# Turning the queries and keys of two attentions through device memory instead of on TensorE

## The chip, the cores and the metric

One NeuronCore of a Trainium2 chip runs the whole program. The metric is device time in microseconds (us) of one execution. The kernel before takes 820.13 us (median of 3 runs, 819.89 to 820.23).

The engines named below are TensorE (PE in the profile; PEld is its weight load), VectorE (DVE), ScalarE (ACT), GpSimd (POOL) and SyncE (SP), which here only starts transfers. Each works through its own list of instructions in order and waits on semaphores.

## The reference, cut to what matters

Two layers of a decoder trunk over 256 tokens of width 2048. Each normalises its input, multiplies it by one wide matrix, feeds the slices of the product to four mixers and multiplies their gated outputs by `w_out`:

```python
for l in range(DEPTH):                       # DEPTH = 2
    u = _rmsnorm(x, ln_g[l]) @ w_in[l]       # 2048 x 6232
    y_a = _gla(...) * silu(g_a)
    y_b = _ssd_mixer(...)
    y_c = _mla(...) * silu(g_c)              # 4 heads, queries and keys of 128 + 64 (the 64 with rope)
    y_d = _dilated_attention(...) * silu(g_d)  # 4 heads of 128, queries and keys with rope
    x = x + concat[y_a, y_b, y_c, y_d] @ w_out[l]
```

Both attentions normalise queries and keys per head, then compute `softmax(mask(q @ k.T * scale)) @ v`, causally, over 256 keys. All data is float32. The queries and keys are made with tokens on the 128 partitions, while the score matmul contracts over the 128 columns of a head, so it needs them turned: columns on partitions, tokens along the free axis.

## The kernel before

**Units.** Both big products run in float32 accuracy from float32r pieces: a weight block is split into `w_hi` (rounded) and `w_lo` (the rest), the activations likewise, and three of the four products are summed in PSUM (`gemm`). The weights come in 144 units per layer, numbered n = 0 to 143 (8 units make one block of 512 or 278 output columns), with 4 more units for the attention's own projections. For each unit four things happen: SP starts a load of 512 KB into one of 4 buffers `raw` (L527); ScalarE copies it to `w_hi` (L1025; "hi n" below); VectorE subtracts for `w_lo` (L1386; "lo n"); TensorE does 8 matmuls with `w_hi` (L702, L703) and 4 with `w_lo` (L711). The load of unit n is started when lo n-4 is done, and hi n waits until TensorE has used unit n-4.

**Everything else is threaded between units.** All other work is written between two units of each engine at a fixed n: `PE_AT` gives n for TensorE's jobs (after unit n), and code of the form `if n == 88:` for the others. The tables `ORDER` name the steps of each engine in order, so that a step can wait for "step X of engine Y". Two pairs of PSUM banks (`pairs`) are used in turn by TensorE's jobs (`bank`), and `LAST_READER` says whose reading frees a pair.

**The attentions.** For the first attention ("mla"), VectorE scales the heads (`mla n`, L1628) and does the rope on the 64-wide part (`mla rope`); then TensorE turns four query heads ("mla qT", after unit 85), four key heads ("mla kT", 86) and the rope parts ("mla rT", 87), each as 8 transposes of 128x128 into PSUM (L874), which ScalarE copies to SBUF (L1213). After unit 89 come the scores of two heads ("mla S 0", L885 and, for the rope part, L891). VectorE takes mask and maximum ("mla max 0", L1659; "mla nmax 0", L1663), ScalarE the exponential ("mla P 0", L1221), TensorE turns the probabilities after unit 92 ("mla PT 0", L900), and TensorE multiplies by the values; so on for the other two heads and for the second attention ("dil"), whose queries and keys are turned after units 95 and 97 and whose first scores come after unit 99. "gated" and "evac 10" belong to the gate of another mixer that passes through at the same place: evac 10 is ScalarE's gate activation with two table loads, directly ahead of ScalarE's copy for "mla rT".

**Turning through memory.** Another way to turn exists already, for the mixers' outputs (`y_squares`) and the state-space output (`ssd_y_squares`): VectorE transposes each 32x32 square in place of its block (`turn_squares`, two instructions for 128x1024, L1355), SP writes the 512 KB to device memory (`squares_out`, L509, at unit at+5) and reads it back in 4 pieces of 128 KB (`squares_back`, L516, at unit at+7), which puts the squares where a full transpose would have them. `SQUARES` names each such tensor with the buffers and its unit "at".

Of the kernel before, what the change touches and what calls it, by code (L numbers as in the profile page):

```python
# [186 lines left out]
for _n in range(8):  # L187
# [3 lines left out]
          "mla kv 1": KV_AT, "ssd Y": 76, "mla qT": 85, "mla kT": 86, "mla rT": 87, "mla S 0": 89, "mla PT 0": 92,  # L191
          "mla S 1": 93, "mla O 0": 94, "dil qT": 95, "mla PT 1": 96, "dil kT": 97, "mla O 1": 98, "dil S 0": 99,
# [7 lines left out]
               "mla cT": ("dve", "mla cT"), "mla qT": ("act", "mla qT"), "mla kT": ("act", "mla kT"), "mla rT": ("act", "mla rT"),  # L200
               "dil qT": ("act", "dil qT"), "dil kT": ("act", "dil kT")}
LAST_READER |= {f"gla level {n}": ("dve", f"gla merge {n}") for n in range(1, 8)}
LAST_READER |= {f"mla {w} {t}": ("act", f"mla {w} {t}") for w in ("q", "kv") for t in range(2)}
for _m in ("mla", "dil"):
    for _i in range(2):
# [25 lines left out]
        "mla cT, ssd Y, mla qT, mla kT, mla rT, "  # L231
        "mla S 0, mla PT 0, mla S 1, mla O 0, dil qT, mla PT 1, dil kT, mla O 1, dil S 0, dil PT 0, dil S 1, dil O 0, "
# [6 lines left out]
        "evac 8, mla kv 0, mla kv 1, mla rs 1 sum, dil rs 0 sum, evac 9, dil rs 1 sum, mla qT, mla kT, evac 10, "  # L239
        "mla rT, mla P 0, ssd rs sum, mla PT 0, mla P 1, evac 11, dil qT, mla PT 1, dil kT, dil P 0, dil PT 0, "  # L240
# [7 lines left out]
        "mla n 0 0, mla n 0 1, ssd yT, mla n 1 0, ssd y squares, mla n 1 1, mla rope products, mla rope, dil n 0 0, dil n 0 1, "  # L248
        "dil n 1 0, dil n 1 1, dil rope 0 products, dil rope 0, dil rope 1 products, dil rope 1, gated 1, mla max 0, "
# [10 lines left out]
def build(nc, xT_d, x_d, pos_d, cols_d, w_d, params_d, gla_w2, gla_b,  # L260
          consts_d, masks_d, out_d):
    ctx = ExitStack()
    with ctx:
# [142 lines left out]
        mqT, mkT = two(A(0, 1024), 4), two(A(1024, 1024), 4)  # L406
# [9 lines left out]
        dqT, dkT = two(A(5632, 1024), 4), two(A(6656, 1024), 4)  # L416
# [87 lines left out]
        def _(sp):  # L504
# [15 lines left out]
            for l in range(DEPTH):  # L520
                for g, n in enumerate(STREAM):
# [109 lines left out]
        def _(pe):  # L631
# [15 lines left out]
            for l in range(DEPTH):  # L647
# [268 lines left out]
                def mla_qT():  # L916
                    pe.wait_ge(*dve("mla rope"))
                    heads_T("mla qT", lambda t, h: mqk[:, t, h, 0:P])

                def mla_kT():  # L920
                    heads_T("mla kT", lambda t, h: mqk[:, t, 4 + h, 0:P])

                def mla_rT():
                    rr = mrr.rearrange("p t (a b) d -> p t a (b d)", b=2)
                    heads_T("mla rT", lambda t, h: rr[:, t, h])
# [3 lines left out]
                       "mla qT": mla_qT, "mla kT": mla_kT, "mla rT": mla_rT}  # L929

                def stages(n):
                    for name in PE_AT:
# [9 lines left out]
                        elif name == "dil qT":  # L942
                            pe.wait_ge(*dve("dil rope 1"))
                            heads_T(name, lambda t, h: dqk[:, t, h])
                        elif name == "dil kT":
                            heads_T(name, lambda t, h: dqk[:, t, 4 + h])
# [38 lines left out]
        def _(act_):  # L985
# [23 lines left out]
            for l in range(DEPTH):  # L1009
# [38 lines left out]
                def evac(b):  # L1048
# [180 lines left out]
                for place, n in enumerate(STREAM):  # L1229
# [72 lines left out]
                    if n == slot("mla qT"):  # L1302
                        heads_T("mla qT", mqT)
                    if n == slot("mla kT"):
                        heads_T("mla kT", mkT)
                    if n == slot("mla rT"):
                        heads_T("mla rT", mrT.rearrange("p a b s -> p (a b) s"))
                    if n == slot("dil qT"):
                        heads_T("dil qT", dqT)
                    if n == slot("dil kT"):  # L1310
                        heads_T("dil kT", dkT)
# [14 lines left out]
        def _(v):  # L1326
# [37 lines left out]
            for l in range(DEPTH):  # L1364
# [329 lines left out]
                for place, n in enumerate(STREAM):  # L1694
# [87 lines left out]
                    for i in range(2):  # L1782
# [72 lines left out]
```

## Time and profile before

| | us |
|---|---|
| median of 3 runs | 820.13 |
| profiled execution | 820.42 |
| its span, first to last instruction | 818.6 |
| TensorE busy in it | 812.2 (99%) |
| VectorE busy | 606.6 (74%) |
| ScalarE busy | 477.2 (58%) |

The granted TensorE clock is at full speed throughout. The span is the time from the first instruction to the last one of the profiled execution; 1.8 us of its device time lie around it. Busy times of TensorE's matmuls overlap, since they are pipelined: how long a job holds the engine is read from the starts of what stands before and behind it. In a row of the timeline the first number is the start, the second the duration of the row (several instructions in a row are merged), and a bracket at its end says how long the engine was idle before it and what ended the wait.

### The profile page before, as it was taken

Reading aid. Unit: us, or ns where it says so; the run is one execution under the profiler, and the core shown is the slowest. Engines: PE = TensorE matmul, PEld = TensorE weight load, DVE = VectorE, ACT = ScalarE, POOL = GpSimd, SP = SyncE. Lnnn points to the kernel's source line nnn. Section 1 sums busy time; section 2 is a strip of 40 time slices with the busy share of each in tenths; the row PEclk is TensorE's granted clock in tenths of the full one; section 3 lists DMA queues with packets and bytes.
Section 4 is the critical chain, followed back from the end, with each engine's and each line's share of the span. In section 5 each row is a group of like instructions: output and inputs, shape, how many; then the busy total and the mean of one; then the engine's idle time right before and its main releaser. Section 6 shows DMA issues by size and latency. Waiting matters only on the chain.

```text
span 818.6 us, 11315 instructions
## 1 busy us (share of the span) xinstructions
PE 812.2 (99%) x4212; PEld 689.6 (84%) x4212; DVE 606.6 (74%) x1074; ACT 477.2 (58%) x786; POOL 52.8 (6%) x64
## 2 busy tenths in 40 slices
PE   8999999999999999999999999999999999999998
PEld 5888888999888888888888888889998888888886
DVE  6678799877896666678965977979769966665552
ACT  6665544777865576433556465457686575664341
POOL 7100000110200000000000000002012000000000
PEclk9999999999999999999999999999999999999999
DMA  9956544576774757655576655456667546676553
GB/s 329 356 203 204 190 134 155 133 230 169 227 222 155 226 161 231 190 194 180 178 258 180 202 159 178 123 154 185 201 179 229 187 152 206 189 224 214 195 190 118
DMA packets 53367, 159.37 MB, mean 195 GB/s; under 512 B 6144, under 2 KB 10928, under 8 KB 53312
## 3 DMA queue, kind: packets, MB, share of 16 engines
q1 hardware_dynamic: 52800, 158.37, 60.9%
q8 instruction: 33, 0.54, 0.3%
q10 hardware_dynamic: 320, 0.21, 0.1%
q14 instruction: 22, 0.18, 0.1%
q0 software_dynamic: 192, 0.07, 0.1%
HBM read 152.32 MB, written 6.31 MB: 194 GB/s over the span
## 4 chain that ended last, share of the span: by engine, by line
PE 91%; DVE 6%; issue 2%; DMA 1%; SPq 0%; ACT 0%; DVEq 0%
PE gemm L711 27%; PE gemm L702 27%; PE gemm L703 26%; DVE arena L1347 3%; DVE w_lo L1386 2%; PE pairs L885 1%; PE pairs L874 1%; DMA raw<-in_weights_dram 1%; PE pairs L861 1%; PE pairs L866 1%; PE pairs L862 1%; PE pairs L832 1%; PE pairs L768 1%; DVE arena L1470 1%; PE pairs L900 1%
## 5 line engine op out<-in xcount | busy, mean ns | idle before, releaser
L1386 DVE TENSOR_TENSOR w_lo<-raw,w_hi 128x1024 fp32r<-128x1024 f32 (+2 forms) x295 | 324.2, 1108 | 156.8 <-ACT w_hi L1025 155.8
L702 PE MATMUL gemm<-w_hi,a_hi 128*128 128x512 f32 (+1 forms) x1144 | 421.2, 374 | 0.5 <-ACT w_hi L1025 0.5
L703 PE MATMUL gemm<-w_hi,a_lo 128*128 128x512 f32 (+1 forms) x1144 | 414.3, 368 | 0.0
L1025 ACT ACTIVATE w_hi<-raw 128x1024 fp32r<-128x1024 f32 (+2 forms) x295 | 281.6, 967 | 201.9 <-PE gemm L711 141.3
L711 PE MATMUL gemm<-w_lo,a_hi 128*128 128x512 f32 (+1 forms) x1144 | 281.8, 368 | 0.2
L702 PEld LDWEIGHTS gemm<-w_hi,a_hi 128*128 128x128 f32 x1144 | 215.2, 188 | 36.2 <-issue 1.5
L703 PEld LDWEIGHTS gemm<-w_hi,a_lo 128*128 128x128 f32 x1144 | 215.3, 188 | 33.1
L711 PEld LDWEIGHTS gemm<-w_lo,a_hi 128*128 128x128 f32 x1144 | 203.3, 188 | 36.6 <-DVE w_lo L1386 1.9
L610 POOL TENSOR_TENSOR st<-st,powers 128x4 f32<-128x4 f32 (+2 forms) x8 | 8.6, 1075 | 431.2 <-ACT arena L1106 213.9
L1058 ACT ACTIVATE u<-gemm,st 128x512 f32<-128x512 f32 (+1 forms) x40 | 22.1, 605 | 19.3 <-PE gemm L711 19.3
L1221 ACT ACTIVATE arena<-arena,st 128x128 f32<-128x128 f32 (+1 forms) x32 | 13.1, 444 | 31.0 <-DVE st L1663 30.9
L1347 DVE STREAM_TRANSPOSE arena<-u 32x256 f32<-32x256 f32 x64 | 27.9, 436 | 1.2
L1347 DVE STREAM_TRANSPOSE u<-x 32x256 f32<-32x256 f32 x48 | 20.9, 436 | 0.6
L1208 ACT ACTIVATE arena<-u 128x192 f32<-128x192 f32 (+1 forms) x64 | 20.6, 330 | 0.8 <-PE pairs L832 0.8
L1551 DVE SCALAR_TENSOR_TENSOR u<-arena,allp,u 128x256 f32<-128x256 f32 x48 | 20.9, 473 | 0.0
L1628 DVE SCALAR_TENSOR_TENSOR u<-u,sth,param_rows 128x192 f32<-128x192 f32 (+1 forms) x64 | 19.9, 377 | 0.0
L1089 ACT ACTIVATE arena<-arena 128x256 f32<-128x256 f32 x16 | 6.8, 424 | 18.0 <-DVE arena L1442 18.0
L1659 DVE CUSTOM_DVE_ANT_0 arena<-pairs,cst 128x128 f32<-128x128 f32 (+1 forms) x32 | 9.5, 352 | 9.4 <-PE pairs L891 3.8
L1213 ACT ACTIVATE arena<-pairs 128x1024 f32<-128x1024 f32 x10 | 10.3, 1028 | 10.1 <-PE pairs L874 10.1
L1338 DVE SCALAR_TENSOR_TENSOR a_lo<-u,allp,a_hi 128x256 fp32r<-128x256 f32 x28 | 14.2, 552 | 2.3 <-ACT a_hi L1006 2.2
L768 PEld LDWEIGHTS pairs<-arena 128*128 128x128 f32 x112 | 14.7, 191 | 1.2
L1510 DVE COPY_PREDICATED o<-lmask,pairs 128x512 f32<-128x512 uint8 x14 | 12.4, 887 | 4.2 <-issue 4.2
(199 smaller groups left out, 628.4 us busy)
## 6 DMA issues: line engine op xcount, KB each, us to landing
raw<-in_weights_dram SPq DMA_DIRECT2D x225, 512.0 KB, 4.1
raw<-in_weights_dram SPq DMA_DIRECT2D x64, 278.0 KB, 3.0
y_squares<-arena SPq DMA_DIRECT2D x6, 512.0 KB, 5.4
arena<-y_squares SPq DMA_DIRECT2D x24, 128.0 KB, 4.2
raw<-in_weights_dram SPq DMA_DIRECT2D x6, 384.0 KB, 3.5
x<-in_x_dram SPq DMA_DIRECT2D x4, 512.0 KB, 6.2
o<-ssd_rows SPq DMA_DIRECT2D x8, 256.0 KB, 4.7
param_rows<-in_params_dram SPq DMA_DIRECT2D x2, 904.0 KB, 7.8
```

The lines of the kernel that those rows point to most:

```text
L702: pe.matmul(acc_t[t], a_hi[:, k, tok[t]], hi, start=k == 0, stop=False)
L703: pe.matmul(acc_t[t], a_lo[:, k, tok[t]], hi, start=False, stop=False)
L711: last = pe.matmul(acc_ps[:, b % 2, t, 0:w], a_hi[:, k, t * P:(t + 1) * P], lo, start=False, stop=k == KT - 1)
L768: last = pe.matmul(to, W[:, p, t * P:(t + 1) * P], Ql[n % 2][:, :, t, p, :], start=True, stop=True)
L1025: A_(w_hi[:, g % SPLIT, 0:c], raw[:, g % RAW, 0:c], ACT.Copy).then_inc(hi_done, 1)
L1058: last = A_(u[:, t, c0 - N_GATE:c0 - N_GATE + w], acc_ps[:, b % 2, t, 0:w], ACT.Copy, scale=xrs[:, t:t + 1])
L1208: last = A_(sq[j % 8] if m == "mla" else sq[:, t, h, :], buf[:, t, 4 * i + h, :], ACT.Square, scale=buf.shape[-1] ** -0.5, accum_out=total ...
L1338: last = v.scalar_tensor_tensor(a_lo[:, k, :], part, gain(l, k), a_hi[:, k, :].bitcast(F32), ALU.mult, ALU.subtract)
L1347: last = v.transpose(to[32 * f:32 * f + 32, :, :, i, :], rows[32 * i:32 * i + 32, :, :, f, :])
L1386: TT(w_lo[:, g % SPLIT, 0:c], raw[:, g % RAW, 0:c], w_hi[:, g % SPLIT, 0:c].bitcast(F32), ALU.subtract).then_inc(split_done, 1)
L1551: last = STT(conv(f), xc[:, f, j:j + S], tap_weight(l, j, f), conv(f), ALU.mult, ALU.add)
L1628: last = STT(buf[:, t, 4 * i + h, :], buf[:, t, 4 * i + h, :], rs[:, j:j + 1], g, ALU.mult, ALU.mult)
```

## The change

The four turns of queries and keys per layer (mla q, mla k, dil q, dil k) leave TensorE. Each becomes a `SQUARES` entry: VectorE transposes the 32x32 squares, SP writes 512 KB out and reads it back in four pieces. The queries are then copied by ScalarE into the layout that the matmul's stationary operand had; the keys are not copied: the score matmul reads them as its moving operand in the layout in which they land, runs of 32 tokens. "mla rT" stays as it was. The places: VectorE's turns at n = 79, 83, 90 and 92; SP's writes at 84, 87, 95 and 97, its reads at 86, 90, 97 and 100; ScalarE's copies of the queries at 88 and 98.

```diff
-          "mla kv 1": KV_AT, "ssd Y": 76, "mla qT": 85, "mla kT": 86, "mla rT": 87, "mla S 0": 89, "mla PT 0": 92,
-          "mla S 1": 93, "mla O 0": 94, "dil qT": 95, "mla PT 1": 96, "dil kT": 97, "mla O 1": 98, "dil S 0": 99,
+          "mla kv 1": KV_AT, "ssd Y": 76, "mla rT": 87, "mla S 0": 89, "mla PT 0": 92,
+          "mla S 1": 93, "mla O 0": 94, "mla PT 1": 96, "mla O 1": 98, "dil S 0": 99,
...
+        OUT, BACK = {"mla k": 4}, {"mla k": 7, "dil k": 8}
+        SQUARES["mla q"] = fold[:, :], A(3072, 1024), 79
+        SQUARES["mla k"] = A(6656, 1024), A(1024, 1024), 83
+        SQUARES["dil q"] = fold[:, :], u[:, 0, 0:1024], 90
+        SQUARES["dil k"] = u[:, 1, 0:1024], A(6656, 1024), 92
...
             def squares_back(l, name):
                 sp.wait_ge(squares_out_done[name], 16 * (l + 1))
+                if name == "mla k":
+                    sp.wait_ge(*reached("dve", l)("mla rope"))
+                if name == "dil k":
+                    sp.wait_ge(*reached("dve", l)("dil rope 1"))
...
-                        if n == at + 5:
+                        if n == at + OUT.get(name, 5):
                             squares_out(l, name)
-                        if n == at + 7:
+                        if n == at + BACK.get(name, 7):
                             squares_back(l, name)
...
-                def scores(m, i, kq, rope):
-                    pe.wait_ge(*act("mla rT" if rope else "dil kT"))
+                def scores(m, i, q, rope):
+                    pe.wait_ge(*act("mla rT" if rope else "dil qT"))
+                    pe.wait_ge(squares_in[f"{m} k"], 16 * 4 * (l + 1))
                     ps = bank()
...
+                    k = SQUARES[f"{m} k"][1].rearrange("p (i h t a) -> p h t i a", i=4, h=4, t=T)
...
-                            last = pe.matmul(ps[:, r, c0:c1], q[:, 2 * i + r, qs], k[:, 2 * i + r, 0:c1 - c0],
+                            last = pe.matmul(ps[:, r, c0:c1], q[:, 2 * i + r, qs], k[:, 2 * i + r, 0:t + 1],
...
+                        if g == 0:
+                            act_.wait_ge(*me("mla qT"))
...
-                def heads_T(name, dst):
-                    act_.wait_ge(*pe(name))
-                    A_(dst, pair_of(name).rearrange("p b (k s) -> p (b k) s", k=2), ACT.Copy).then_inc(*signal("act", name))
+                def heads_T(name, to):
+                    act_.wait_ge(squares_in[name], 16 * 4 * (l + 1))
+                    act_.wait_ge(*dve("mla rope" if name == "mla q" else "dil rope 1"))
+                    A_(to.rearrange("p h (t i a) -> p i (h t) a", t=T, i=4), SQUARES[name][1].rearrange("p (i c a) -> p i c a", i=4, a=32), ACT.Copy).then_inc(*signal("act", name + "T"))
...
+                def head_squares(name):
+                    m, i = name[:3], "qkr".index(name[4])
+                    if name == "dil q":
+                        v.wait_ge(squares_out_done["mla q"], 16 * (l + 1))
+                    if name == "mla q" and l:
+                        v.wait_ge(squares_out_done["dil q"], 16 * l)
+                    v.wait_ge(*me(f"mla n {i} 1" if m == "mla" else f"dil rope {i}"))
+                    heads = (mqk if m == "mla" else dqk)[:, :, 4 * i:4 * i + 4, 0:P]
+                    turn_squares(SQUARES[name][0], heads).then_inc(*sig(f"{name} squares"))
...
                 def rope_products(name, after, x1, x2, tmp, nh, hd, step):
+                    if name == "dil rope 0":
+                        v.wait_ge(squares_out_done["mla k"], 16 * (l + 1))
```

How this stands in VectorE's list between the products of dil rope 1 and mla max 0 (units 90 to 92), before. L1386 is lo, L1642 and L1643 the sums of the rope, L1400 "gated", L1655 the first instruction of mla max 0:

```order
L1638 TENSOR_TENSOR arena<-u,sincos 128x512
L1386 TENSOR_TENSOR w_lo<-raw,w_hi 128x1024 [waits hi_done]
L1642 TENSOR_TENSOR u<-arena 128x2x4x64 [waits dve_stages]
L1643 TENSOR_TENSOR u<-arena 128x2x4x64
L1400 TENSOR_TENSOR o<-arena 128x4x8x32 [waits ssd_y_squares_in,act_stages]
L1386 TENSOR_TENSOR w_lo<-raw,w_hi 128x1024 [waits hi_done]
L1655 MEMSET st 128x1 [waits dve_stages,pe_stages]
```

And now, with lo at L1390, the rope's sums at L1660 and L1661, "gated" at L1404, the first of mla max 0 at L1673:

```order
L1656 TENSOR_TENSOR arena<-u,sincos 128x512
L1359 STREAM_TRANSPOSE fold<-u 128x4x4x32 [waits dve_stages,mla_q_squares_out]
L1359 STREAM_TRANSPOSE fold<-u 128x4x4x32
L1390 TENSOR_TENSOR w_lo<-raw,w_hi 128x1024 [waits hi_done]
L1660 TENSOR_TENSOR u<-arena 128x2x4x64 [waits dve_stages]
L1661 TENSOR_TENSOR u<-arena 128x2x4x64
L1404 TENSOR_TENSOR o<-arena 128x4x8x32 [waits ssd_y_squares_in,act_stages]
L1390 TENSOR_TENSOR w_lo<-raw,w_hi 128x1024 [waits hi_done]
L1359 STREAM_TRANSPOSE u<-u 128x4x4x32 [waits dve_stages]
L1359 STREAM_TRANSPOSE u<-u 128x4x4x32
L1673 MEMSET st 128x1 [waits dve_stages,pe_stages]
```

Two pairs of transposes (dil q and dil k) now stand ahead of mla max 0; the pairs of mla q and mla k stand further up in the same list, behind lo 79 and lo 83.

ScalarE's list from hi 88 to the copy of mla rT, before. L1025 is hi, L1213 the copies of the turned heads out of PSUM, L1064 and L1067 evac 10:

```order
L1025 ACTIVATE w_hi<-raw 128x1024 [waits unit_used,weights_in_0]
L1213 ACTIVATE arena<-pairs 128x1024 [waits pe_stages]
L1025 ACTIVATE w_hi<-raw 128x1024 [waits unit_used,weights_in_1]
L1213 ACTIVATE arena<-pairs 128x1024 [waits pe_stages]
L1025 ACTIVATE w_hi<-raw 128x1024 [waits unit_used,weights_in_2]
L1064 ACT_TABLE_LOAD [waits unit_used]
L1064 ACTIVATE arena<-gemm,st 128x512 [waits unit_used]
L1064 ACTIVATE arena<-gemm,st 128x512
L1067 ACT_TABLE_LOAD
L1213 ACTIVATE arena<-pairs 128x1024 [waits pe_stages]
```

And now (hi is L1024, the queries' copy L1217, evac 10 L1066 and L1069, the copy of mla rT L1221):

```order
L1024 ACTIVATE w_hi<-raw 128x1024 [waits unit_used,weights_in_0]
L1217 ACTIVATE arena<-arena 128x4x8x32 [waits dve_stages,mla_q_squares_in]
L1024 ACTIVATE w_hi<-raw 128x1024 [waits unit_used,weights_in_1]
L1024 ACTIVATE w_hi<-raw 128x1024 [waits unit_used,weights_in_2]
L1066 ACT_TABLE_LOAD [waits unit_used,act_stages]
L1066 ACTIVATE arena<-gemm,st 128x512 [waits unit_used]
L1066 ACTIVATE arena<-gemm,st 128x512
L1069 ACT_TABLE_LOAD
L1221 ACTIVATE arena<-pairs 128x1024 [waits pe_stages]
```

One of the two copies of turned heads is gone, and the other waits for a transfer where it waited for TensorE.

## Rows read from the trace of the kernel before

**Rows 1.** The profile's page: engines' busy time, and the chain that ended last.

```profile
PE 812.2 (99%) x4212; PEld 689.6 (84%) x4212; DVE 606.6 (74%) x1074; ACT 477.2 (58%) x786; POOL 52.8 (6%) x64
...
PE 91%; DVE 6%; issue 2%; DMA 1%; SPq 0%; ACT 0%; DVEq 0%
```

**Rows 2.** Timeline of TensorE, layer 1, units 84 to 86 and 95, 96.

```profile
228.62 1.07 PE L711 MATMUL gemm<-w_lo,a_hi 128*128 128x512 f32 x4
...
231.34 1.07 PE L711 MATMUL gemm<-w_lo,a_hi 128*128 128x512 f32 x4
232.25 1.03 PE L874 MATMUL pairs<-cst,u 128*128 128x128 f32 x8
...
234.96 1.07 PE L711 MATMUL gemm<-w_lo,a_hi 128*128 128x512 f32 x4
...
268.21 1.07 PE L711 MATMUL gemm<-w_lo,a_hi 128*128 128x512 f32 x4
...
271.85 1.08 PE L711 MATMUL gemm<-w_lo,a_hi 128*128 128x512 f32 x4
```

**Rows 3.** Timeline of VectorE, layer 1, units 81 to 98: lo, mla max 0, y's squares.

```profile
214.81 1.22 DVE L1386 TENSOR_TENSOR w_lo<-raw,w_hi 128x1024 fp32r<-128x1024 f32 x1 [0.35 <-ACT w_hi L1025]
...
224.57 1.21 DVE L1386 TENSOR_TENSOR w_lo<-raw,w_hi 128x1024 fp32r<-128x1024 f32 x1
...
244.82 1.22 DVE L1386 TENSOR_TENSOR w_lo<-raw,w_hi 128x1024 fp32r<-128x1024 f32 x1 [0.79 <-ACT w_hi L1025]
...
249.44 0.28 DVE L1659 CUSTOM_DVE_ANT_0 arena<-pairs,cst 128x128 f32<-128x128 f32 x1
...
268.91 1.30 DVE L1355 STREAM_TRANSPOSE arena<-o 128x512 f32<-128x512 f32 x2
270.13 1.18 DVE L1386 TENSOR_TENSOR w_lo<-raw,w_hi 128x1024 fp32r<-128x1024 f32 x1
```

**Rows 4.** Timeline of ScalarE: units 89 to 94 of layer 1, last row layer 2.

```profile
235.17 1.06 ACT L1025 ACTIVATE w_hi<-raw 128x1024 fp32r<-128x1024 f32 x1 [0.81 <-DMA raw<-in_weights_dram]
...
242.81 1.03 ACT L1213 ACTIVATE arena<-pairs 128x1024 f32<-128x1024 f32 x1
...
250.87 0.40 ACT L1221 ACTIVATE arena<-arena,st 128x128 f32<-128x128 f32 x1 [5.14 <-DVE st L1663]
...
252.65 1.99 ACT L1025 ACTIVATE w_hi<-raw 128x1024 fp32r<-128x1024 f32 x2
...
656.61 2.00 ACT L1025 ACTIVATE w_hi<-raw 128x1024 fp32r<-128x1024 f32 x2
```

**Rows 5.** Timeline of TensorE, layer 1, scores and turned probabilities, units 89 to 100.

```profile
245.84 1.48 PE L885 MATMUL pairs<-arena 128*128 128x128 f32 x8
...
256.46 0.81 PE L900 MATMUL pairs<-cst,arena 128*128 128x128 f32 x6
257.03 0.48 PE L702 MATMUL gemm<-w_hi,a_hi 128*128 128x512 f32 x1
...
283.88 1.48 PE L885 MATMUL pairs<-arena 128*128 128x128 f32 x8
```

**Rows 6.** Timeline of SyncE, layer 1: weight loads 87 and 88, and five from 89 on.

```profile
222.27 3.87 SPq L527 DMA_DIRECT2D raw<-in_weights_dram  x2
...
229.17 10.47 SPq L527 DMA_DIRECT2D raw<-in_weights_dram  x5
```

**Rows 7.** DMA issues: KB each, and median us from issue to landing.

```profile
y_squares<-arena SPq DMA_DIRECT2D x6, 512.0 KB, 5.4
arena<-y_squares SPq DMA_DIRECT2D x24, 128.0 KB, 4.2
```

**Rows 8.** Matmuls of L768 and L885: ns least, median, most; first and last start.

```profile
L768 PE MATMUL pairs<-arena x112: 272/275/275, 89.2 to 532.0; 128*128 128x128 f32 x112
...
L885 PE MATMUL pairs<-arena x64: 272/327/382, 245.8 to 701.9; 128*128 128x128 f32 x32, 128*128 128x256 f32 x32
```

**Rows 9.** Source view of L1595, the state-space output's transposes of squares, four per layer.

```profile
L1595 DVE STREAM_TRANSPOSE arena<-u x8: 399/406/439, 217.3 to 622.2; 128x256 f32<-128x256 f32 x8
```

More of the change, by code:

```diff
@@ L199 @@
                "ssd cum": ("dve", "ssd row"), "ssd gcol": ("act", "ssd gcol"), "ssd CB": ("dve", "ssd CB"), "ssd Y": ("dve", "ssd yT"),
-               "mla cT": ("dve", "mla cT"), "mla qT": ("act", "mla qT"), "mla kT": ("act", "mla kT"), "mla rT": ("act", "mla rT"),
-               "dil qT": ("act", "dil qT"), "dil kT": ("act", "dil kT")}
+               "mla cT": ("dve", "mla cT"), "mla rT": ("act", "mla rT")}
 LAST_READER |= {f"gla level {n}": ("dve", f"gla merge {n}") for n in range(1, 8)}
@@ L230 @@
         "gla level 6, gla level 7, gla out, ssd cum, ssd gcol, ssd CB, ssd xs, "
-        "mla cT, ssd Y, mla qT, mla kT, mla rT, "
-        "mla S 0, mla PT 0, mla S 1, mla O 0, dil qT, mla PT 1, dil kT, mla O 1, dil S 0, dil PT 0, dil S 1, dil O 0, "
+        "mla cT, ssd Y, mla rT, "
+        "mla S 0, mla PT 0, mla S 1, mla O 0, mla PT 1, mla O 1, dil S 0, dil PT 0, dil S 1, dil O 0, "
         "dil PT 1, dil O 1, yT 3",
@@ L247 @@
         "conv 0 3, conv 0 4, conv 0 5, ssd CB, mla cn, ssd E 0, ssd xdt, mla cT, ssd E 1, ssd M 0, ssd M 1, "
-        "mla n 0 0, mla n 0 1, ssd yT, mla n 1 0, ssd y squares, mla n 1 1, mla rope products, mla rope, dil n 0 0, dil n 0 1, "
-        "dil n 1 0, dil n 1 1, dil rope 0 products, dil rope 0, dil rope 1 products, dil rope 1, gated 1, mla max 0, "
+        "mla n 0 0, mla n 0 1, ssd yT, mla q squares, mla n 1 0, ssd y squares, mla n 1 1, mla k squares, mla rope products, mla rope, dil n 0 0, dil n 0 1, "
+        "dil n 1 0, dil n 1 1, dil rope 0 products, dil rope 0, dil rope 1 products, dil q squares, dil rope 1, gated 1, dil k squares, mla max 0, "
         "mla nmax 0, mla max 1, mla nmax 1, y 1, mla ri 0, mla O 0, y 1 squares, y 0, y 0 squares, mla ri 1, mla O 1, dil max 0, "
@@ L405, in build @@
         mtmp = [A(i * 512, 512, "p (t h d) -> p t h d", t=T, h=8) for i in range(4)]
-        mqT, mkT = two(A(0, 1024), 4), two(A(1024, 1024), 4)
+        mqT = two(A(0, 1024), 4)
         mrT = A(2048, 1024, "p (a b s) -> p a b s", a=2, b=2)
@@ L415, in build @@
         dtmp = [A(5632 + i * 512, 512, "p (t h d) -> p t h d", t=T, h=4) for i in range(4)]
-        dqT, dkT = two(A(5632, 1024), 4), two(A(6656, 1024), 4)
+        dqT = two(A(5632, 1024), 4)
         def stat(a, n):
@@ L914, in values, with mla_rT @@
                     last.then_inc(*signal("pe", f"{m} O {i}"))
-                def mla_qT():
+                def mla_rT():
                     pe.wait_ge(*dve("mla rope"))
[L918 to L923, printed above, removed]
                     rr = mrr.rearrange("p t (a b) d -> p t a (b d)", b=2)
@@ L928, in _ @@
                        "gla out": gla_out, "ssd xs": ssd_xs, "ssd cum": ssd_cum, "ssd gcol": ssd_gcol, "ssd CB": ssd_CB, "ssd Y": ssd_Y, "mla cT": mla_cT,
-                       "mla qT": mla_qT, "mla kT": mla_kT, "mla rT": mla_rT}
+                       "mla rT": mla_rT}
                 def stages(n):
@@ L941, in stages @@
                             gla_level(i)
[L942 to L946, printed above, removed]
                         elif name.startswith("mla S"):
-                            scores("mla", i, (mqT, mkT), True)
+                            scores("mla", i, mqT, True)
                         elif name.startswith("dil S"):
-                            scores("dil", i, (dqT, dkT), False)
+                            scores("dil", i, dqT, False)
                         elif name.startswith("mla PT"):
@@ L1301, in _ @@
                         head_sums("dil", 1)
[L1302 to L1305, printed above, removed]
+                    if n == 88:
+                        heads_T("mla q", mqT)
+                    if n == 98:
+                        heads_T("dil q", dqT)
                     if n == slot("mla rT"):
[L1307 to L1311, printed above, removed]
+                        mla_rT()
                     for m in ("mla", "dil"):
@@ L1777, in _ @@
                         ssd_y_squares()
+                    for name in ("mla q", "mla k"):
+                        if n == SQUARES[name][2]:
+                            head_squares(name)
                     if n == 83:
@@ L1790, in _ @@
                             rope_sums(f"dil rope {i}", b[:, :, :, 0:64], b[:, :, :, 64:128], dtmp)
+                    for name in ("dil q", "dil k"):
+                        if n == SQUARES[name][2]:
+                            head_squares(name)
                     for m in ("mla", "dil"):
```

8 lines of the change are left out of this document (4 added, 4 removed), and 2 rows, old and new, of the table ORDER.

## The prediction

> **What bounds the kernel now.** I read the page first. TensorE is busy 99% of the span and 91% of the chain that ended last [rows 1], so time taken from TensorE's list comes off the end, unless TensorE then waits for somebody. VectorE's 74% and ScalarE's 58% are averages over stages. I therefore read next the timelines of TensorE, VectorE and ScalarE in the stretch that is edited, units 79 to 100 of layer 1 (214 to 285 us). There VectorE's list is nearly solid: between lo 81 and mla max 0 (214.81 to 249.44) it is idle only where a bracket says so, once for 0.79 us, and 0.35 us just ahead [rows 3]. TensorE is still not held up, since lo and hi run ahead of it: lo 84 ends at 224.57 + 1.21 = 225.78, and TensorE's first use of it is at 228.62 [rows 2, 3], 2.84 us later. A gain on TensorE here has to fit through these margins.
>
> **What is taken from TensorE.** A unit's `w_lo` matmuls start 231.34 - 228.62 = 2.72 us after those of the unit before. With eight transposes between, the distance is 234.96 - 231.34 = 3.62 us for mla q, and 271.85 - 268.21 = 3.64 us for dil q [rows 2]. So a turn costs 0.90 and 0.92 us. All four turns go: 2 x 0.90 = 1.80 us for mla q and k, 2 x 0.92 = 1.84 us for dil q and k, 3.64 us per layer, 7.28 us in both. That is the ceiling.
>
> **What VectorE gets.** Each turn is a pair of transposes of 128x512. From the start of such a pair to what follows it is 270.13 - 268.91 = 1.22 us [rows 3]. Four are 4.88 us per layer. The other bound is the state-space output's form, 4 instructions of 406 ns [rows 9], which overlap no better than end to end: 1.62 us a turn, 6.50 us in four. I take 1.22, as shape and helper are the same. Lower than that nothing in the trace suggests.
>
> All four stand ahead of mla max 0 in an in-order list that was full. The two idle times swallow 0.35 + 0.79 = 1.14 us (hi 81 and hi 91, for which VectorE waited, do not move by as much), so mla max 0 comes 4.88 - 1.14 = 3.74 us later than 249.44. Its input doesn't hold it: mla S 0 begins at 245.84 [rows 5].
>
> **The new wait.** ScalarE waits for this maximum: mla P 0 starts at 250.87 after 5.14 us of idleness, ended by VectorE, and hi 93 follows at 252.65, two hi in 1.99 us [rows 4]. 3.74 us later, mla P 0 ends at 256.39 and hi 93 at 257.39. TensorE turns these probabilities (mla PT 0) at 256.46 and starts unit 93 at 257.03 [rows 5]. With 1.80 us taken off ahead it would be ready at 254.66 and 255.23. So it waits 256.39 - 254.66 = 1.73 us at mla PT 0, then reaches unit 93 at 256.96 and waits 0.43 us more for hi 93. The 1.80 us of the first two turns are used up here, and 0.36 us besides. Behind this, mla S 1, and with it mla max 1, follows TensorE again, and in layer 2 the same place looks the same (hi 93 at 656.61 [rows 4]).
>
> **The other edits up to there.** lo 84 is the tightest on the way: two pairs less 0.35 us make it 2.09 us later, which leaves 0.75 of 2.84 us. lo 85 to lo 89 keep more, though TensorE comes up to 1.80 us earlier there. On ScalarE one copy of 1.03 us goes; the other reads SBUF, which I cost as a hi, 1.0 us [rows 4]. The copy of mla rT (242.81, done 243.84) allows mla S 0, which began 2.0 us after; ready 1.80 us earlier, TensorE gets a wait there if hi 89, hi 90 or evac 10 slip, but up to 1.73 us of such a wait is only taken early from the wait at mla PT 0. The keys: a write takes 5.4 us to land, a read back 4.2 [rows 7]. SP writes mla k behind load 87, which was issued at 222.27 [rows 6] and slips with lo 83 by some 2 us (about 224.5 us), reads it about 232 to 234 behind load 90 (before: the second of the five loads from 229.17 on [rows 6], again some 2 us later), and it lands by about 238 to 239, before mla S 0. What is queued behind these SP instructions are weight loads. Load 89, issued at 229.17 right behind a read back, let hi 89 start at 235.17, with 0.81 us of waiting for the DMA [rows 4, 6]: 6.0 us. I cost the slip of load 89 (behind two more transfers, to about 231.2) as covered: hi 89 would end near 238.4, and VectorE, 2.09 us later itself, wants it near 240.1.
>
> Whether the score matmul is slower with keys in runs of 32 is not shown. Bounds: nothing, as the moving operand of L768, made of two runs of 64, takes 275 ns, against 272 for a contiguous one of the same 128 columns [rows 8]; or twice the time, 1.41 us more (mla S 0's eight matmuls less the last one's tail of 0.07, from 1.48 [rows 5]) for each of eight score jobs, 11.3 us. I take nothing: the near row has the same kind of operand. A gain I exclude, since no column fewer is read.
>
> The order of the two engines may also be weighed by a rule. In these rows a 128x128 block costs TensorE 0.90 / 8 = 0.113 us, and VectorE 1.22 / 8 = 0.153 us for its squares alone [rows 2, 3]. The Trainium skill, "VectorE: DVE Perf Modes", Rules for kernel authors, says to turn a 128x128 block on TensorE where the result may go to PSUM, which speaks against this change, and the trace agrees in direction: 4.88 us added to save 3.64. Its section The three transpose paths has 390 ns on TensorE and 311 ns on VectorE (in bf16); by these, as an estimate, a layer would save 12.5 us on TensorE for 10.0 us on VectorE, which the durations here contradict.
>
> **Behind mla S 1.** dil q and k save 1.84 us. dil S 0 stands at 283.88 [rows 5], 282.4 after the change. The keys' squares are written behind load 97, which waits for lo 93 (about 259.7), and the read of dil q is issued ahead of it: written by 267, read back 4.2 us plus four issues later, by 273. ScalarE's copy of dil q lies near 274. Both are in time by 8 us, so this half stays.
>
> **Sum.** Per layer 3.64 - 1.73 - 0.43 = 1.48 us; two layers 2.96 us. The profiled execution, 820.42 us (818.6 of span and 1.8 around it), becomes 817.5. The median of the runs is 0.29 us below the profiled one, so I forecast 817.2. With the dearer turns (1.62 us), 1.6 us more per layer is waited: 820.4.
>
> **Rivals.**
> 1. The whole gain: 820.13 - 7.28 = 812.9. It needs VectorE's 3.74 us to vanish, that is, mla P 0 to start no later than 250.87 - 1.80. VectorE's 26% of idleness speaks for it, the solid rows up to 249.44 against it. 0.11; half-way cases, 814 to 815.5, are in it.
> 2. Weight loads late by a little: the reads of mla q, the state-space output and mla k lie within 14 us, and loads between them land late. Each us by which hi 89 or hi 90 slips past what VectorE wants goes through mla max 0 on to TensorE, twice. At 0.8 to 2.3 us per layer past the 1.7 us of cover the result is within 0.2% of before: 819 to 821. For it speaks that ScalarE already waits for a load at hi 89; against, that the transfers of `y_squares` at 102 to 114 do the same without a wait of TensorE. 0.19.
> 3. Slower: the same queue, with load 89 taking twice its 6.0 us. Issued at 231.2 it lands at 243.2, hi 89 ends at 244.2, lo 89 is 4.1 us late beyond the shift. Per layer 4.1 - 1.48 = 2.6 us lost, 825.4. It decides from 1.48 us of further lateness on. The strided keys at twice the time would give 828.5, from 0.37 us per score job on. Together 0.12.
> 4. The keys might need a copy or more matmuls after all; the score job is listed with the same four matmuls, so I give it no chance.
>
> **Chances.** My case 0.58, rival 1 0.11, rival 2 0.19, rival 3 0.12. About 0.2% (1.64 us) is what a measurement of this kernel can tell from no change: faster means below 818.5. My case's own range is 815.8 to 818.4 (turns and hand-overs of plus or minus 0.7 us per layer). Faster: 0.58 + 0.11 = 0.69; the same 0.19; slower 0.12. The range, 814.2 to 820.6, takes in rival 2 and the dearer turns.
>
> **What would show it.** Right: TensorE without L874 out of `u`, units 85 to 87 closing up by 0.9 us each; on VectorE no idle time at lo 81 and lo 91, mla max 0 some 3.7 us later in the list; an idle TensorE of about 2 us split between mla S 0, mla PT 0 and unit 93, released by ScalarE, in both layers; no wait at dil S 0. Wrong: no such idle time (rival 1), ScalarE's hi 87 to 90 waiting for loads for longer than now (rivals 2 and 3), or L885's duration above 327 ns (strided keys).

## The result, and the profile after

The changed kernel takes 821.69 us (median of 12 runs, 818.58 to 823.97), the kernel before, beside it, 820.21 us (12 runs, 819.74 to 820.57). The ratio is 1.0019, 95% interval 1.0012 to 1.0026: slower by 1.5 us, where 3.0 us of gain were forecast. The runs also lie 5.4 us apart, those of the kernel before 0.8 us.

The profiled execution took 819.80 us, 818.0 of them span. Its page, against [rows 1]: TensorE has 4.8 us less to do, VectorE 9.5 us more, and the chain that ended last, 91% TensorE before, is 80% TensorE, with VectorE and the DMA in place of the rest.

```profile
PE 807.4 (99%) x4148; PEld 683.9 (84%) x4148; DVE 616.1 (75%) x1090; ACT 473.1 (58%) x782; POOL 54.2 (7%) x64
...
PE 80%; DVE 9%; DMA 4%; ACT 3%; issue 3%; SPq 1%; DVEq 0%
```

The 4.8 us can be misread: 7.28 us of turns went, and a slower clock gave part of it back. TensorE's timeline shows the slower clock and the wait ahead of it, mla S 0 of layer 1 first (the number in brackets is the idle time ahead), then the same job of dil S 0, then mla S 0 of layer 2:

```profile
245.81 2.35 PE L895 MATMUL pairs<-arena 128*128 128x128 f32 x8 [2.14 <-ACT arena L1221]
248.08 1.65 PE L901 MATMUL pairs<-arena 64*128 64x128 f32 x8
...
283.60 1.48 PE L895 MATMUL pairs<-arena 128*128 128x128 f32 x8
...
650.99 1.58 PE L895 MATMUL pairs<-arena 128*128 128x128 f32 x8 [3.19 <-ACT arena L1221]
```

TensorE waits 2.14 and 3.19 us for L1221, ScalarE's copy of mla rT, and nowhere else in the layers. In layer 1 the eight matmuls then take 2.35 us; undisturbed it is 1.48, as L885's was [rows 5]. The windows of this stretch name the clock (columns as headed):

```profile
core 0: us, PE busy (x) PEld busy (x) DVE busy (x) ACT busy (x) POOL busy (x), PEclk, DMA share, GB/s
225.00:235.00 10.00, 10.00 (x46) 8.29 (x45) 10.00 (x21) 3.28 (x4) 0.00 (x0) 1.00 1.03 314
235.00:240.00 5.00, 5.00 (x28) 4.23 (x27) 5.00 (x10) 2.14 (x3) 0.00 (x0) 1.00 1.09 272
240.00:245.00 5.00, 3.66 (x17) 2.69 (x15) 5.00 (x8) 4.94 (x6) 0.00 (x0) 1.00 0.97 320
...
246.50:249.50 3.00, 3.00 (x14) 1.78 (x12) 2.92 (x5) 1.14 (x2) 0.00 (x0) 0.50 0.32 27
250.00:254.00 4.00, 4.00 (x19) 3.29 (x19) 3.94 (x14) 0.00 (x0) 0.00 (x0) 1.00 0.93 341
```

```profile
225.00:235.00 10.00, 10.00 (x50) 8.38 (x49) 10.00 (x23) 3.56 (x4) 0.00 (x0) 1.00 0.84 256
235.00:240.00 5.00, 5.00 (x30) 4.26 (x29) 5.00 (x8) 4.10 (x4) 0.00 (x0) 1.00 0.51 194
240.00:245.00 5.00, 5.00 (x26) 4.18 (x25) 4.21 (x7) 4.96 (x7) 0.00 (x0) 1.00 0.70 210
```

How the full queue leads to the wait is in ScalarE's timeline, hi 89 to the copy of mla rT, then mla P 0:

```profile
237.49 1.06 ACT L1024 ACTIVATE w_hi<-raw 128x1024 fp32r<-128x1024 f32 x1 [1.64 <-DMA raw<-in_weights_dram]
239.78 1.06 ACT L1024 ACTIVATE w_hi<-raw 128x1024 fp32r<-128x1024 f32 x1 [1.22 <-DMA raw<-in_weights_dram]
240.86 1.28 ACT L1066 ACT_TABLE_LOAD   x1
242.15 1.27 ACT L1066 ACTIVATE arena<-gemm,st 128x512 f32<-128x512 f32 x2
243.44 1.28 ACT L1069 ACT_TABLE_LOAD   x1
244.73 1.02 ACT L1221 ACTIVATE arena<-pairs 128x1024 f32<-128x1024 f32 x1
...
254.01 0.40 ACT L1229 ACTIVATE arena<-arena,st 128x128 f32<-128x128 f32 x1 [6.37 <-DVE st L1681]
```

hi 90 waits for its weight load until 239.78, and 3.9 us of evac 10 follow; only then comes the copy. In layer 2 hi 90 starts at 644.96 after 1.58 us of such a wait, and the copy at 649.92. SP's queue tells why the load is late (columns: start, time to issue):

```profile
221.00 1.75 SPq L525 DMA_DIRECT2D arena<-mla_q_squares  x4
222.80 0.43 SPq L513 DMA_DIRECT2D ssd_y_squares<-arena  x1
223.28 0.43 SPq L536 DMA_DIRECT2D raw<-in_weights_dram  x1
223.75 1.07 SPq L513 DMA_DIRECT2D mla_k_squares<-arena  x1
227.22 0.33 SPq L536 DMA_DIRECT2D raw<-in_weights_dram  x1
229.14 1.74 SPq L525 DMA_DIRECT2D arena<-ssd_y_squares  x4
230.93 0.90 SPq L536 DMA_DIRECT2D raw<-in_weights_dram  x2
231.95 2.44 SPq L525 DMA_DIRECT2D arena<-mla_k_squares  x4
```

Load 90, issued at 231.4 as the second of the pair, lands at 239.75: 8.35 us (10.1 in layer 2). Between 221 and 231 us a read back, a write, a load, a write, a load and a read back of 512 KB each stand ahead of the pair.

In 11 of the 12 runs the time follows the mean granted clock: 0.998 in four (819.8 to 820.9 us), 0.996 or 0.995 in five (821.6 to 823.2), 0.994 in two (823.8 and 824.0). The exception is the fastest run, 818.6 us at 0.997: the clock is not all that differs. One stretch as the above costs 1.6 us: in layer 1 unit 90 begins 249.67 - 245.81 = 3.86 us after mla S 0, where the first experiment below has 246.66 - 244.40 = 2.26.

### The profile page after: what moved, and what is told of

The parts are those of the page before. It is cut to its first block, busy times and chain, and to the rows that moved or that the text cites. A ratio compares the mean times of both kernels' runs of the same rounds, so it can differ in the third digit from the quotient of the medians.

```text
span 818.0 us, 11248 instructions
## 1 busy us (share of the span) xinstructions
PE 807.4 (99%) x4148; PEld 683.9 (84%) x4148; DVE 616.1 (75%) x1090; ACT 473.1 (58%) x782; POOL 54.2 (7%) x64
## 4 chain that ended last, share of the span: by engine, by line
PE 80%; DVE 9%; DMA 4%; ACT 3%; issue 3%; SPq 1%; DVEq 0%
PE gemm L720 24%; PE gemm L711 24%; PE gemm L712 23%; DVE w_lo L1390 3%; DVE arena L1351 3%; DMA raw<-in_weights_dram 2%; PE pairs L895 1%; DMA ssd_y_squares<-arena 1%; PE pairs L871 1%; PE pairs L875 1%; PE pairs L870 1%; DMA mla_q_squares<-fold 1%; DVE u L1632 1%; PE pairs L777 1%; DVE arena L1474 1%
## 5 line engine op out<-in xcount | busy, mean ns | idle before, releaser
L1390 DVE TENSOR_TENSOR w_lo<-raw,w_hi 128x1024 fp32r<-128x1024 f32 (+2 forms) x295 | 325.5, 1113 | 152.6 <-ACT w_hi L1024 151.3
L1024 ACT ACTIVATE w_hi<-raw 128x1024 fp32r<-128x1024 f32 (+2 forms) x295 | 281.5, 967 | 220.6 <-PE gemm L720 139.0
L895 PE MATMUL pairs<-arena 128*128 128x128 f32 (+1 forms) x64 | 12.8, 345 | 5.3 <-ACT arena L1221 5.3
L895 PEld LDWEIGHTS pairs<-arena 128*128 128x128 f32 x64 | 9.9, 198 | 7.1 <-ACT arena L1221 6.2
L777 PEld LDWEIGHTS pairs<-arena 128*128 128x128 f32 x112 | 14.7, 191 | 1.2
L777 PE MATMUL pairs<-arena 128*128 128x128 f32 x112 | 14.8, 275 | 0.0
```

What stands on the lines that cost most here:

```text
L777: last = pe.matmul(to, W[:, p, t * P:(t + 1) * P], Ql[n % 2][:, :, t, p, :], start=True, stop=True)
L1024: A_(w_hi[:, g % SPLIT, 0:c], raw[:, g % RAW, 0:c], ACT.Copy).then_inc(hi_done, 1)
L1390: TT(w_lo[:, g % SPLIT, 0:c], raw[:, g % RAW, 0:c], w_hi[:, g % SPLIT, 0:c].bitcast(F32), ALU.subtract).then_inc(split_done, 1)
```

## The experiments

**Theory 1**: TensorE waits at mla S 0 for the copy of mla rT, which stands in ScalarE's list behind hi 90 and so behind load 90, late in a full queue; the idle time brings the clock down with it. **Theory 2**: the loss is VectorE's four added turns ahead of mla max 0.

**1. The copy of mla rT first.**

```diff
-        "evac 8, mla kv 0, mla kv 1, mla rs 1 sum, dil rs 0 sum, evac 9, dil rs 1 sum, mla qT, evac 10, "
-        "mla rT, mla P 0, ssd rs sum, mla PT 0, mla P 1, evac 11, dil qT, mla PT 1, dil P 0, dil PT 0, "
+        "evac 8, mla kv 0, mla kv 1, mla rs 1 sum, dil rs 0 sum, evac 9, dil rs 1 sum, mla qT, mla rT, evac 10, "
+        "mla P 0, ssd rs sum, mla PT 0, mla P 1, evac 11, dil qT, mla PT 1, dil P 0, dil PT 0, "
```

> The changed kernel with one edit: ScalarE copies the turned mla rT ahead of hi 90 and evac 10 instead of behind them. Theory 1 (TensorE waits at mla S 0 for this copy, which stands behind hi 90 and so behind the late weight load 90): the copy ends about 240 us into the span in layer 1, the idle time of TensorE at mla S 0 (2.14 us in layer 1, 3.19 us in layer 2 in the changed kernel) goes or falls under 0.3 us, some of it turns up again as a wait at mla PT 0 and unit 93 because mla P 0 still waits for VectorE, and the time falls from 821.7 us to 817 to 818. Theory 2 (VectorE's added turns ahead of mla max 0 are the whole loss, the wait at mla S 0 only takes it early): the waits move to mla PT 0 and unit 93 with the same sum, and the time stays within 0.5 us of 821.7.

Measured: 819.17 us (816.42 to 820.47, 12 runs), 0.9983 of before [0.9975, 0.9992]. mla S 0 begins without a wait in both layers, and the wait sits at mla PT 0, 1.47 us in layer 1 and 1.72 in layer 2:

```profile
256.65 0.87 PE L910 MATMUL pairs<-cst,arena 128*128 128x128 f32 x6 [1.47 <-ACT arena L1229]
...
659.16 0.87 PE L910 MATMUL pairs<-cst,arena 128*128 128x128 f32 x6 [1.72 <-ACT arena L1229]
```

Theory 1 has the place right: 2.5 us came back. The time is 1.2 us above what it expected, most of it because the clock now falls behind this wait: 0.998 in eight runs (818.9 to 820.5), 0.999 in one (820.0), 1.0 in three (816.4, 818.2, 818.2). In the profiled execution, behind the 1.72 us of layer 2:

```profile
656.00:660.00 4.00, 2.28 (x13) 1.50 (x11) 1.18 (x9) 2.76 (x10) 0.00 (x0) 1.00 0.32 118
660.00:664.00 4.00, 3.93 (x11) 3.09 (x11) 2.78 (x3) 4.00 (x12) 1.18 (x2) 0.59 0.41 133
```

**2. A quarter of the traffic.**

```diff
+                cut = 256 if name[:3] == "mla" else 1024
-                sp.dma_start(squares_d[name], SQUARES[name][0]).then_inc(squares_out_done[name], 16)
+                sp.dma_start(squares_d[name][:, 0:cut], SQUARES[name][0][:, 0:cut]).then_inc(squares_out_done[name], 16)
...
-                for f in range(4):
+                for f in range(1 if name[:3] == "mla" else 4):
```

> The changed kernel, with the trips of mla q and mla k over device memory cut to a quarter: 128 KB out and 128 KB back each in place of 512 KB. It leaves out three quarters of the turned queries and keys of the first attention; all instructions of TensorE, VectorE and ScalarE stay. Theory 1 (the two trips delay weight load 90, that delays hi 90, that the copy of mla rT, that mla S 0): load 90 lands 2 to 3 us earlier than its 8.35 us (layer 1) and 10.1 us (layer 2), ScalarE's wait at hi 90 goes, TensorE's wait at mla S 0 falls under 1 us, and the time is 817 to 818.5 us. Theory 2 (VectorE's added turns are the loss): VectorE's list is as long as before, so the time stays at 821 to 822.

Measured: 816.92 us (816.51 to 816.99, 5 runs), just under the range that theory 1 expected, clock 0.999 or 1.0 in each. Load 90 took 6.8 us in layer 1. No wait at mla S 0; at mla PT 0 1.35 and 1.44 us, and then a short one for hi 93 that no bracket shows. Unit 93 begins 256.99 - 256.04 = 0.95 us after mla PT 0, as soon as hi 93 has ended; before it was 257.03 - 256.46 = 0.57 [rows 5]. That is 0.38 us, and about as much in layer 2 and in experiment 1. hi 93 in ScalarE's timeline, then TensorE's:

```profile
255.89 1.99 ACT L1025 ACTIVATE w_hi<-raw 128x1024 fp32r<-128x1024 f32 x2
...
256.04 0.87 PE L911 MATMUL pairs<-cst,arena 128*128 128x128 f32 x6 [1.35 <-ACT arena L1230]
256.99 0.50 PE L712 MATMUL gemm<-w_hi,a_hi 128*128 128x512 f32 x1
```

VectorE's list is as long as in the changed kernel, so theory 2 falls: its turns alone cost somewhat less than the forecast had put there, and the traffic is the rest.

**3. The dil turns behind mla max 0.**

```diff
-        SQUARES["dil q"] = fold[:, :], u[:, 0, 0:1024], 90
-        SQUARES["dil k"] = u[:, 1, 0:1024], A(6656, 1024), 92
+        SQUARES["dil q"] = fold[:, :], u[:, 0, 0:1024], 93
+        SQUARES["dil k"] = u[:, 1, 0:1024], A(6656, 1024), 94
```

> The changed kernel with the turns of dil q and dil k on VectorE moved from ahead of mla max 0 to behind it (units 93 and 94; their writes, reads and ScalarE's copy of the queries move by as much). Theory 1 (the wait at mla S 0 for the copy of mla rT is the loss, and mla max 0 has slack behind it): mla max 0 no longer waits for 2.4 us of turns, but TensorE still waits 2.1 and 3.2 us at mla S 0; only what is waited at unit 93 and at mla PT 0 (under 0.5 us per layer) comes back, 820.5 to 822 us. Theory 2 (the turns ahead of mla max 0 are the loss): some 2 us per layer come back, 817 to 818 us.

Measured: 820.92 us (818.35 to 826.68, 12 runs), as theory 1 expected. mla P 0 still comes late, since mla S 0 does: in the profiled execution load 90 took 10.4 us in layer 1, and

```profile
249.25 2.93 PE L895 MATMUL pairs<-arena 128*128 128x128 f32 x8 [4.79 <-ACT arena L1221]
```

Nothing ahead of load 90 is edited here, so how long this wait is differs from one execution to the next.

**4 and 5. TensorE kept busy during the wait**, with 16 transposes of the identity, then with 40.

```diff
+                    if (m, i) == ("mla", 0):
+                        ps = bank()
+                        for j in range(16):
+                            pe.transpose(ps[:, j // 4 % 2, j % 4 * P:(j % 4 + 1) * P], ident, ident)
                     pe.wait_ge(*act("mla rT" if rope else "dil qT"))
```

> The changed kernel with 16 further transposes of the identity on TensorE (16 x 0.113 us = 1.8 us per layer), placed ahead of mla S 0 and not waiting for anything, so that most of TensorE's idle time there is filled. Clock theory (of the loss, the part that differs from run to run comes from a fall of the granted clock to 0.5 after TensorE's idle time at mla S 0, 3.4 us long in the profiled execution): the clock stays at 1.0 after mla S 0, the median falls to about 819 us, and the runs lie closer together than 818.6 to 824.0 us, though TensorE has 3.6 us more to do. Plain wait theory (the wait is the loss and the clock plays no part): the fill fits into the wait, 821.5 to 822.5 us, with the runs as far apart as without it.

> The changed kernel with 40 transposes of the identity ahead of mla S 0 instead of 16: 40 x 0.113 = 4.5 us per layer, longer than the waits of 2.1 and 3.2 us there. With 16 the profiled execution took 817.8 us at a clock of 1.0, with 2.45 and 2.73 us between unit 89 and mla S 0; 4.5 us in both layers is 3.8 us more, 821.6 us. Clock theory (idle time of TensorE at mla S 0 is what makes the granted clock fall, and these falls make the runs differ): no idle time is left there, the clock is 0.999 or 1.0 in nearly all runs, and they lie within 1 us. If the falls come from something else in this stretch (the transfers, the state of the chip), the runs spread over 5 us or more as with 16.

Measured with 16: 819.16 us (816.63 to 824.70, 12 runs): 2.5 us faster than without, though TensorE has more to do. The median came as the clock theory had it, the runs did not close up, they lie 8.1 us apart: at a clock of 1.0 six lie at 816.6 to 818.6 us, one at 0.999 took 819.7, and five at 0.998 to 0.996 took 821.1 to 824.7. The fill is shorter than the wait even in the profiled execution, at a clock of 1.0, where 0.54 and 0.82 us are left at mla S 0. With 40: 821.33 us (820.99 to 822.58, 11 runs) at a clock of 1.0 in all eleven; 1.6 us between the fastest and the slowest instead of the 1 us expected, and of 5.4 without. The transposes run straight into mla S 0, which then takes its 1.48 us:

```profile
245.00 4.53 PE L891 MATMUL pairs<-cst 128*128 128x128 f32 x40
249.36 1.48 PE L900 MATMUL pairs<-arena 128*128 128x128 f32 x8
```

The traffic is the same in both. So behind mla S 0 the clock falls for TensorE's idle time and not for the transfers, and the wait there, by its length and by the falls behind it, is most of what made the runs differ; both are shown. A wait is not enough, though (behind the 3.19 us of layer 2 the changed kernel's clock stayed at 1.0), and not every fall has a wait that is known: the kernel before, with no wait in the layers of its profiled execution, has a mean clock of 0.998 in two of its 29 runs beside experiments 1 to 4 (821.1 and 821.4 us).

**6 and 7. One attention alone.** The kernel before, with the entries of one attention moved to `SQUARES` and the other's turns left on TensorE; first dil:

```diff
+        SQUARES["dil q"] = fold[:, :], u[:, 0, 0:1024], 90
+        SQUARES["dil k"] = u[:, 1, 0:1024], A(6656, 1024), 92
```

and then mla:

```diff
+        SQUARES["mla q"] = fold[:, :], A(3072, 1024), 79
+        SQUARES["mla k"] = A(6656, 1024), A(1024, 1024), 83
```

> The kernel before with the second attention's half of the change alone: dil q and dil k turned over device memory, mla q and mla k on TensorE as before. Theory 1 (the loss arises at the first attention's scores, from the two mla trips in the queue ahead of the weight loads): this half keeps all of its 2 x 1.84 us, TensorE waits nowhere in the layers, and the time is 820.2 - 3.7 = 816.5 us, with runs as close together as those of the kernel before. Rival (trips over device memory cost in either place, or keys read in runs of 32 do): 818 us or more.

> The kernel before with the first attention's half of the change alone: mla q and mla k turned over device memory, dil q and dil k on TensorE as before. Theory 1: 3.6 us come off TensorE, but with two turns less on VectorE ahead of mla max 0 nothing waits behind mla S 0, so that the waits at mla S 0 (5.3 us in both layers of the changed kernel) are lost in full, and a fall of the clock or two at 1.7 us each with them: 823.5 to 825.5 us, slower than the kernel before and than the changed kernel. Theory 2 (VectorE's four turns ahead of mla max 0 are the loss): only two of them are left, they fit, and the time is 816.5 to 817.5 us.

Measured: dil alone 816.62 us (816.06 to 816.69, 5 runs), 3.70 us faster than the 820.32 beside it, where 2 x 1.84 = 3.68 were expected. mla alone 826.91 us (819.80 to 828.06, 7 runs), ratio 1.0066 [1.0042, 1.0090]: the loss sits there. It is 1.4 us above the expected range; the one run at a clock of 1.0 took 819.8, the others at 0.997 to 0.994 took 823.8 to 828.1. The profiled one (823.84) waited 3.64 and 1.42 us at mla S 0, and the clock fell behind the first; how long the slower ones waited, no trace shows.

```profile
247.71 2.80 PE L893 MATMUL pairs<-arena 128*128 128x128 f32 x8 [3.64 <-ACT arena L1228]
```

**8. Both moves**, of experiments 1 and 3.

> The changed kernel with both edits: ScalarE's copy of mla rT ahead of hi 90 and evac 10, and VectorE's turns of dil q and dil k behind mla max 0. If the two waits behind each other (mla S 0 for the copy, mla PT 0 for mla P 0) are all that the change lost, neither is left: mla P 0 starts 2.4 us earlier than with the first edit alone, which takes away its 1.5 and 1.7 us of waiting at mla PT 0, the clock has no cause to fall, and the time is 820.2 - 7.28 = 812.9 to 814.5 us. If the weight loads themselves are late enough to hold TensorE at a unit (hi 90, lo 90 or hi 91), a wait at a unit shows, and the time is 815 to 817 us.

Measured: 815.20 us (813.92 to 815.57, 5 runs), clock 0.999 or 1.0. The waits of 1.47 and 1.72 us at mla PT 0 are gone. What is left was not on the list of expectations: in layer 1 mla S 0 waits 0.82 us for the keys, whose last piece took 10.65 us and landed at 244.63. Some 0.3 us at mla PT 0 and 0.4 at unit 93 are left there too: load 90 is still late, hi 91 with it, lo 91 waits 1.32 us for that, and mla max 0 and mla P 0 follow.

```profile
244.72 1.55 PE L895 MATMUL pairs<-arena 128*128 128x128 f32 x8 [0.82 <-issue]
```

**9 and 10. The state-space output's read back out of the way**, alone and on top of experiment 8:

```diff
-        OUT, BACK = {"mla k": 4}, {"mla k": 7, "dil k": 8}
+        OUT, BACK = {"mla k": 4}, {"mla k": 7, "dil k": 8, "ssd y": 9}
```

> The changed kernel with only the read back of the state-space output moved, from ahead of weight load 89 to behind the read back of mla k. Nothing is left out and no instruction of TensorE, VectorE or ScalarE moves. Theory 1 (load 90 is late because of the reads that stand ahead of it in the queue): hi 90 starts 1 to 2 us earlier, the wait at mla S 0 shrinks from 2.1 and 3.2 us to about 1 and 2 us, part of it turns up at mla PT 0, where mla P 0 is as late as before, the clock falls in fewer runs, and the time is 817.5 to 819.5 us. Rival (VectorE's added turns, or the traffic as such): 821.7 us.

> The kernel with both edits (copy of mla rT first, dil turns behind mla max 0; 815.2 us, of which 0.82 us is a wait of mla S 0 for the last piece of the keys, landed 10.7 us after its issue), and the read back of the state-space output moved from ahead of weight load 89 to behind the read back of mla k. Theory 1 (what is late here is what stands behind 512 KB of reads in the queue): loads 89 and 90 and the keys land 1 to 2 us earlier, the wait of mla S 0 goes, the output's own pieces land by 244 us, 5 us ahead of their use on VectorE, and the time is 813 to 814.5 us. Rival (the queue's order does not matter, only what is in flight): the keys land where they did, 815 us.

Measured alone: 817.06 us (816.25 to 818.03, 5 runs), 0.9962 of before [0.9948, 0.9976]. One number was changed, and 4.6 us came back, 0.4 us more than theory 1 expected at most; one run of the five has a clock of 0.998 (818.0 us), the others 1.0. hi 90 starts 1.0 us earlier than in the changed kernel, in an execution whose TensorE stands 0.9 us later there (mla rT at 238.08 instead of 237.17), and the wait at mla S 0 is 0.22 us in layer 1 (0.75 in layer 2), less than expected, with 1.03 us at mla PT 0 (0.51). ScalarE's hi 90 and TensorE's two waits in layer 1:

```profile
238.76 1.06 ACT L1024 ACTIVATE w_hi<-raw 128x1024 fp32r<-128x1024 f32 x1 [2.62 <-DMA raw<-in_weights_dram]
...
244.80 1.58 PE L895 MATMUL pairs<-arena 128*128 128x128 f32 x8 [0.22 <-ACT arena L1221]
...
256.65 0.88 PE L910 MATMUL pairs<-cst,arena 128*128 128x128 f32 x6 [1.03 <-ACT arena L1229]
```

In experiment 8, load 90 took 9.50 us and the last piece of the keys 10.65; in experiment 10, 7.46 and 7.80. The Trainium skill, "DMA: Bandwidth & Descriptors", Two DMAs through the same engine are not ordered, says that within one queue of one DMA engine transfers start in order, but that a later one can complete before an earlier one has finished writing. These landings agree with it: what came to stand ahead of the moved read back lands sooner, and in experiment 8 load 90 (241.59) still lands after the first pieces of the keys, issued behind it (from 240.47 on).

Measured on top of both moves: 812.89 us (812.47 to 812.96, 4 runs), ratio 0.9911 [0.9898, 0.9925], clock 1.0 in each. The chain that ended last is TensorE's again, with no wait of it in the layers:

```profile
PE 91%; DVE 7%; issue 2%; DMA 0%; ACT 0%; SPq 0%; DVEq 0%
```

In TensorE's timeline mla S 0 and mla PT 0 of layer 1 stand without a bracket:

```profile
244.00 1.48 PE L895 MATMUL pairs<-arena 128*128 128x128 f32 x8
...
254.62 0.82 PE L910 MATMUL pairs<-cst,arena 128*128 128x128 f32 x6
```

It beats both kernels: 7.15 us below the 820.04 beside it, of 7.28 us that the turns took on TensorE. The prediction weighed a rule of the Trainium skill ("VectorE: DVE Perf Modes", Rules for kernel authors) that keeps such turns on TensorE. Here, once nothing waits for the added work, the measurement decides against it.

## Why the prediction was wrong

- **The ceiling** was right: 7.28 us forecast, 7.15 measured where no wait is left.
- **VectorE's chain** was right. mla max 0 came 3.7 us later in the list by the forecast and started at 252.58 instead of 249.44 in an execution that was 0.5 us ahead there: 3.67. Without a wait at mla S 0 (experiments 1 and 2), TensorE waits 1.35 to 1.72 us at mla PT 0, where 1.73 was forecast, and 0.4 us more at unit 93, where 0.43 was. With the loads earlier the time comes to the forecast 817.2 us: 816.92 in experiment 2, 817.06 in experiment 9, where part of the wait still is at mla S 0.
- **The keys** in runs of 32 cost nothing: 1.48 us for L895 at 283.60 as for L885 [rows 5]. **The dil half** was kept whole (experiment 6).
- **The step that failed** is the wait at mla S 0. The text saw it coming "if hi 89, hi 90 or evac 10 slip" and put nothing for it into the sum, since "up to 1.73 us of such a wait is only taken early" and the slip of load 89 was "covered". Load 89 was: issued at 230.93, it took 6.5 us where 6.0 were carried over, and hi 89 ended at 238.55, where 238.4 was forecast. Load 90 right behind it was not priced in the sum. It took 6.8 us in the kernel before, with one trip over device memory in the queue, and 8.35 and 10.1 us with three. And the cover was judged at lo 89 on VectorE, where there was some, instead of at the copy of mla rT on ScalarE, which has hi 90 and 3.9 us of evac 10 ahead of it: there the text's own figures leave 2.0 - 1.80 = 0.2 us. The copy started 1.92 us later (244.73 instead of 242.81), and TensorE waited 2.14 and 3.19 us. That 1.73 us of it were only taken early held: nothing is waited at mla PT 0 and unit 93 behind it, so that 5.3 us of waits stand against the 4.3 of the sum.
- **What was not in the sum**: an idle TensorE was costed at its length. In the profiled execution a wait of 2.14 us cost 1.6 us more by the clock. That execution took 819.8 us, 2.3 more than the 817.5 forecast for it: 5.3 - 4.3 = 1.0 us of waits and 1.6 of clock, less 0.5 us by which it was ahead at unit 80, make 2.1. The median is 1.9 us above it. Runs near it have a mean clock of 0.996, 0.002 below the profiled one, which over 820 us is 1.6 us. That these runs waited longer too is likely, but only one execution has a trace.
- **Rivals** 2 and 3 had the cause, late loads, and their sign came: hi 87, 88, 89 and 90 of layer 1 wait 3.76, 2.46, 1.64 and 1.22 us for their loads, where it was 1.81, 2.20, 0.81 and nothing. But they sent it through lo and mla max 0 on VectorE; it went through hi 90 to ScalarE's copy. The range was also too narrow for rival 2: 2.3 us per layer on 817.2 is 821.8, not 821, and the range, said to take it in, ended at 820.6.

What stays open: what decides whether the clock falls behind a wait, and what made the time differ in runs of one clock (816.4 and 818.2 us at 1.0 in experiment 1).

## What to carry to other kernels

When a change adds transfers, take the latency of every load behind them from a stretch in which the DMA engines are as full as they will be; the last load of the group decides, not the first. Then follow each late load down the in-order list of the engine that takes it, to the first small instruction that TensorE needs: moving that one instruction ahead, or a read back that nobody needs yet behind, gave back 2.5 and 4.6 us here, more than the change had lost. Wait time on TensorE can have a second price, the clock, so a gain that leaves waits on it may come out smaller than the sum of their lengths says.
